# Two sets of six SBUF places for the weights of the extra expert pairs, and these pairs placed behind static pairs 3 to 10

## The reference

```python
def hier_moe(h, w_rg, b_rg, w_re, b_re, w_gate, w_up, w_down):
    g_idx = argmax(h @ w_rg + b_rg)                     # one of 4 groups of 8 experts
    e_in = (h @ w_re + b_re) of the chosen group
    top_v, top_i = top_k(e_in, 2)                       # two experts for each token
    combine = onehot(g_idx) * (g_w * softmax(top_v) at top_i)
    for every expert e:                                 # 32 experts, hidden width 256
        act = silu(h @ w_gate[e]) * (h @ w_up[e]) * combine[:, e]
        out = out + act @ w_down[e]
    return out                                          # x = x + out
```

## Time and profile before

| | us |
|---|---|
| median of 3 runs | 1676.72 (1676.46 to 1681.14) |
| span of the profiled execution | 1676.2 |
| PE busy | 1552.3 (93%) |
| DVE, ACT, POOL busy | 915.1, 761.6, 151.8 |
| 1400 to 1677 us: the router and the experts | 277 |

### The profile page before, as it was taken

The page is one execution under the profiler, slowest core; times in us unless marked ns, Lnnn a source line. Parts: engine busy times, 40 slices in busy tenths (PEclk is TensorE's granted clock), DMA queues, the critical chain, the costliest instruction groups (busy, mean ns, idle before and its releaser), DMA issues.

```text
span 1676.2 us, 23054 instructions
## 1 busy us (share of the span) xinstructions
PE 1552.3 (93%) x9664; PEld 1253.1 (75%) x9664; DVE 915.1 (55%) x1298; ACT 761.6 (45%) x1201; POOL 151.8 (9%) x202
## 2 busy tenths in 40 slices
PE   7999999999999999997999998989999999686676
PEld 6888888788887888875788888977999977333332
DVE  5545577745464554567644545796876765510102
ACT  6444554544364444466644444556755653111111
POOL 0000000100010000011100001050001000232320
PEclk9999999999999999999999999999999999798988
DMA  7555545555557455532345554432553248999996
GB/s 290 176 188 189 201 164 178 187 179 193 181 178 269 169 177 185 191 126 101 137 178 188 189 177 160 151 126 101 176 174 104 101 176 325 369 415 413 414 416 274
DMA packets 55366, 347.23 MB, mean 207 GB/s; under 512 B 10516, under 2 KB 10916, under 8 KB 15168
## 3 DMA queue, kind: packets, MB, share of 16 engines
q1 hardware_dynamic: 47520, 333.17, 53.8%
q0 software_dynamic: 7744, 12.61, 2.2%
HBM read 396.34 MB, written 9.96 MB: 242 GB/s over the span
## 4 chain that ended last, share of the span: by engine, by line
PE 78%; DVE 8%; DMA 7%; ACT 4%; issue 3%; POOL 1%; SPq 0%; DVEq 0%; POOLq 0%; ACTq 0%
PE A L424 31%; PE Y L454 20%; PE A L377 6%; PE A L362 4%; PE A L2985 4%; DMA raw<-experts,extra 2%; PE Y L3006 2%; DMA raw_whi<-experts 2%; DVE wlo L322 1%; PE A L438 1%; PE Y L393 1%; DMA raw<-stream 1%; ACT whi L311 1%; PE A L721 1%; DVE xn L521 1%
## 5 line engine op out<-in xcount | busy, mean ns | idle before, releaser
L322 DVE TENSOR_TENSOR wlo<-raw,whi 128x2048 fp32r<-128x2048 f32 (+1 forms) x226 | 496.9, 2206 | 246.2 <-ACT whi L311 245.3
L311 ACT ACTIVATE whi<-raw 128x2048 fp32r<-128x2048 f32 (+1 forms) x226 | 415.7, 1848 | 93.1 <-DMA raw<-stream 93.1
L424 PE MATMUL A<-whi,xh 128*128 128x512 f32 x768 | 308.5, 402 | 5.1 <-DVE wlo L322 5.1
L424 PE MATMUL A<-whi,xl 128*128 128x512 f32 x768 | 301.4, 392 | 0.0
L424 PE MATMUL A<-wlo,xh 128*128 128x512 f32 x768 | 300.8, 392 | 0.0
L424 PEld LDWEIGHTS A<-whi,xh 128*128 128x128 f32 x768 | 144.9, 189 | 34.2 <-DVE wlo L322 5.9
L424 PEld LDWEIGHTS A<-whi,xl 128*128 128x128 f32 x768 | 144.6, 188 | 31.7
L424 PEld LDWEIGHTS A<-wlo,xh 128*128 128x128 f32 x768 | 145.1, 189 | 28.4
L454 PE MATMUL Y<-whi,hh 128*128 128x512 f32 x352 | 140.8, 400 | 1.2 <-DVE hl L801 1.2
L454 PE MATMUL Y<-wlo,hh 128*128 128x512 f32 x352 | 139.4, 396 | 0.0
L454 PE MATMUL Y<-whi,hl 128*128 128x512 f32 x352 | 139.3, 396 | 0.0
(11 more groups left out here) (464 smaller groups left out, 2791.1 us busy)
## 6 DMA issues: line engine op xcount, KB each, us to landing
raw<-stream SPq DMA_DIRECT2D x216, 1024.0 KB, 4.9
raw_whi<-experts SPq DMA_DIRECT2D x39, 1024.0 KB, 26.5
raw<-experts SPq DMA_DIRECT2D x22, 1024.0 KB, 28.5
far<-experts SPq DMA_DIRECT2D x17, 1024.0 KB, 18.7
raw_x<-experts SPq DMA_DIRECT2D x12, 1024.0 KB, 28.5
xn<-experts SPq DMA_DIRECT2D x6, 1024.0 KB, 28.3
gains<-post_rows POOLq DMA_DIRECT2D x6, 512.0 KB, 4.7
far<-sums_at SPq DMA_DIRECT2D x4, 512.0 KB, 5.8
```

Source lines behind the costliest of these rows:

```text
L311: nc.scalar.activation(whi[:, n % RING, c], raw[:, n % RING, c], ACT.Copy).then_inc(hi_ready.sem, 1)
L322: nc.vector.tensor_tensor(wlo[:, n % RING, c], raw[:, n % RING, c], whi[:, n % RING, c].bitcast(F32), ALU.subtract).then_inc(lo_ready.sem, 1)
L424: ins = nc.tensor.matmul(bank, lhsT=lhs[:, kk, tok(t)], rhs=w[:, k, :], start=(kk == 0 and q == 0), stop=(kk == KD - 1 and q == 2))
```

## The change

The extra pairs move to stand behind static pairs 3 to 10, so at q = 4, 6, 8, ..., 18: five static pairs (11 to 15) come after the last of them. Their weights alternate between two sets of six places. Set 0 is the old one. Set 1 is `raw_whi` 2 to 4 and `ring_seam`, three places that span the end of `raw` and the beginning of `whi`; its places 6, 8, 10, 11, 14 and 16 are taken from the static loads, for which 8 places are left instead of 14. The first loads of both sets wait for the last static user of the set, every later one for the down product of the extra pair two before it. The final read of `sums_at` waits for the second-last extra pair, the last to use set 0.

```diff
-        if e in (3, 5, 6, 8, 9, 11, 12, 13):
+        if e in (3, 4, 5, 6, 7, 8, 9, 10):
             order.append(EXPERTS // 2 + len(order) - e - 1)
...
-        kept = (2, 3, 4, 5, 7, 9)
-        extra_place = [far[:, 0:3, :], raw[:, first_raw:first_raw + 3, :]]
...
-        around = [i for i in range(PLACES) if i not in kept]
+        kept = ((2, 3, 4, 5, 7, 9), (6, 8, 10, 11, 14, 16))
+        ring_seam = nc.alloc_sbuf_tensor_at("ring_seam", [P, 3, SLOT], F32, offset=place_whi - 4 * SLOT)
+        extra_place = [[far[:, 0:3, :], raw[:, first_raw:first_raw + 3, :]],
+                       [raw_whi[:, first_raw:first_raw + 3, :], ring_seam]]
...
+        around = [i for i in range(PLACES) if i not in kept[0] + kept[1]]
...
                 def weights(i):
-                    if i == 0:
-                        pool.wait_ge(slot_done.sem, first_static + static[kept[-1]] + 1)
+                    if i < 2:
+                        pool.wait_ge(slot_done.sem, first_static + static[kept[i][-1]] + 1)
                     else:
-                        pool.wait_ge(slot_done.sem, done(extra_pairs[i - 1], 2))
+                        pool.wait_ge(slot_done.sem, done(extra_pairs[i - 2], 2))
...
-                    if q == 1:
-                        weights(0)
-                    elif q in extra_pairs[:-1]:
-                        weights(extra_pairs.index(q) + 1)
+                    if q in (1, 2):
+                        weights(q - 1)
+                    elif q in extra_pairs[:-2]:
+                        weights(extra_pairs.index(q) + 2)
...
-                sp.wait_ge(slot_done.sem, done(extra_pairs[-1], 2))
+                sp.wait_ge(slot_done.sem, done(extra_pairs[-2], 2))
```

More of the change, by code:

```diff
@@ L238, in build @@
         stored = signal("stored")
-        scaled_in = signal("scaled_in")
         rows_out = signal("rows_out")
@@ L260, in build @@
         expert_loaded = [signal(f"expert_loaded{i}") for i in range(PLACES - RING)]
-        extra_loaded = signal("extra_loaded")
+        extra_loaded = [signal(f"extra_loaded{i}") for i in range(2)]
         expert_out = signal("expert_out")
@@ L2630, in build @@
         place_loaded += [next(free) for i in range(3)]
-        kept = (2, 3, 4, 5, 7, 9)
-        extra_place = [far[:, 0:3, :], raw[:, first_raw:first_raw + 3, :]]
-        assert first_raw + 3 <= RING and len(places) == PLACES
-        around = [i for i in range(PLACES) if i not in kept]
+        kept = ((2, 3, 4, 5, 7, 9), (6, 8, 10, 11, 14, 16))
+        ring_seam = nc.alloc_sbuf_tensor_at("ring_seam", [P, 3, SLOT], F32, offset=place_whi - 4 * SLOT)
+        extra_place = [[far[:, 0:3, :], raw[:, first_raw:first_raw + 3, :]],
+                       [raw_whi[:, first_raw:first_raw + 3, :], ring_seam]]
+        assert first_raw == 2 and RING == 6 and len(places) == PLACES and place_whi == place + 4 * RING * SLOT
+        around = [i for i in range(PLACES) if i not in kept[0] + kept[1]]
         static = [m for m in range(6 * PAIRS) if not is_extra(PIECES[m // 2][0])]
@@ L2646, in build @@
             if m not in loaded:
-                place_of[m] = extra_place[m % 2][:, part, :]
-                loaded[m] = extra_loaded.sem, 32 * (ORDER[q] - EXPERTS // 2 + 1)
+                i = ORDER[q] - EXPERTS // 2
+                place_of[m] = extra_place[i % 2][m % 2][:, part, :]
+                loaded[m] = extra_loaded[i % 2].sem, 32 * (i // 2 + 1)
         def load_expert(sp, m):
@@ L2883, in sparse_experts @@
             SENT = PAIRS - 2
-            yk = [extra_place[0][:, i, :].rearrange("p (t d) -> p t d", t=NT) for i in range(2)]
+            yk = [extra_place[0][0][:, i, :].rearrange("p (t d) -> p t d", t=NT) for i in range(2)]
             extra_pairs = [q for q in range(PAIRS) if is_extra(q)]
@@ L2937, in weights @@
                 def weights(i):
-                    if i == 0:
-                        pool.wait_ge(slot_done.sem, first_static + static[kept[-1]] + 1)
+                    if i < 2:
+                        pool.wait_ge(slot_done.sem, first_static + static[kept[i][-1]] + 1)
                     else:
-                        pool.wait_ge(slot_done.sem, done(extra_pairs[i - 1], 2))
+                        pool.wait_ge(slot_done.sem, done(extra_pairs[i - 2], 2))
                     for j in range(2):
-                        pool.indirect_dma_start(extra_place[j].rearrange("p a c -> p (a c)"), None, expert_rows,
+                        pool.indirect_dma_start(extra_place[i % 2][j].rearrange("p a c -> p (a c)"), None, expert_rows,
                                                 bass.IndirectOffsetOnAxis(choice.extra[:, 2 * i + j:2 * i + j + 1], 0),
-                                                bounds_check=P * EXPERTS - 1, oob_is_err=False).then_inc(extra_loaded.sem, 16)
+                                                bounds_check=P * EXPERTS - 1, oob_is_err=False
+                                                ).then_inc(extra_loaded[i % 2].sem, 16)
                 def scatter(q):
```

## The result

| | before | after |
|---|---|---|
| median | 1677.8 us (1675.2 to 1681.3, 14 runs) | 1684.1 us (1679.0 to 1688.4, 14 runs) |
| span of the profiled execution | 1676.2 us | 1684.0 us |

The ratio is 1.003 with a 95% interval of 1.002 to 1.0041, so some 5 us, with 3.4 to 6.9 as its ends; the two medians are 6.3 us apart. Forecast were 5.0 us, so it agrees within the noise, and not to the tenth. The profiled execution of the changed kernel took 1685.7 us in all, 1.6 over its own median, so its trace shows the loss a little too large.

A forecast was written before the change was run, and what follows sets the result against it. The slowest DMA engine's stream of static loads was taken as the bound; 0 + 0.5 + 4.5 + 0 = +5.0 us on 1676.2 gave 1681.2, with 0.5 for the median 1681.7; range 1676.5 to 1688.

The forecast's parts named there:

- The bound is the slowest DMA engine's stream: Experts: the slowest of 16 DMA engines, at 2.79 us a static load, sets the time, not the mean share.
- the faster rival: Tail: a ring of 8 keeps the engines together, so the stream ends sooner; 1670.9 us, chance 0.13.
- Extra weights' waits: TensorE's 23.6 us of waits for extra weights: all but the first should go, for a gain of 0.
- Late restart: Start of the experts: static load 22 goes out at 1462.00 instead of 1456.00; +4.5 us, from 2 to 6.
- The step's two deductions: Start of the experts: from 6.0 us, 0.6 off for earlier small gaps and 0.9 for rows done in the gap.
- the 4 to 6 us that were given for the last landing: End of the stream: sign that the last static load lands 4 to 6 us later than 1664.3.
- Tail: After the last landing: extra pairs earlier gain 0, at most 1.3 us, against a cold merge; +0.5, from -1.3 to +3.
- Ring of eight: Alternation of static and extra pairs: eight places keep the loads queued, 16.7 us a period against TensorE's 13.3; 0.
- my margin of 4 us: After the restart: the queue reaches to 1486.3, and the next loads' first packets come at 1482.
- POOL's wait: Extra pair 1's weights wait in POOL's queue for static load 16, ahead of a gather needed two pairs later; 0.
- The sign by which the rival was to be told: End of the stream: the engines' spread shrinks from 18 us to less than half.

The follow-up runs named there:

- e6_no_rows: Kernel before with the bounds of the experts' gathers and scatters set to 0, so nearly no row is moved; 1666.7 us, ratio 0.9932.
- e10_old_order_second_use: Changed kernel with the old order of pairs, static loads 22 to 25 using places 6, 8, 10 and 11 a second time; 1678.8 us, ratio 1.0005.
- e4_before_held: Kernel before with one wait added: static load 22 is issued only when static load 12 is done; 1683.7 us, ratio 1.003.
- e3_second_use: Changed kernel, static loads 22 to 25 reusing places 6, 8, 10, 11; extra pair 1's weights wait for load 25, not 16; 1691.4 us, ratio 1.0069.
- e1_old_order_two_sets: Changed kernel with the old positions of the extra pairs, two sets and eight places kept; 1684.0 us, ratio 1.0035.
- e7_spread_rows: Kernel before with one table changed, so that each expert's tokens are spread over its 32 row places; 1674.3 us, ratio 0.9974.

## Why the prediction was right, point by point

- **The bound is the slowest DMA engine's stream.** Shown: 12.4 us from the last static packet to the end in 11 of 13 kernels, and 4 MB less make it about 10 us shorter. The 73 loads took 1672.1 - 1469.9 = 202.2 us after, 2.77 each (1469.9 is s = 22's landing, 4.9 us behind its issue); the forecast took 2.79. The 2.4 us a load by which the faster rival had the stream end some 28 us sooner were not seen: even without rows (e6_no_rows) it was 193.4 us for 74 loads, 2.6 each.
- **Extra weights' waits: 0.** Shown: 23.6 us of waits became 0.2 with no gain, and e10_old_order_second_use has the second set without the late restart and stays at 1.0005.
- **Late restart: +4.5.** Shown. As measured in e4_before_held: +5.9 at the start, less 1.5 caught up, is +4.4. The step's two deductions (0.6 for the small gaps of before, 0.9 for rows done in the gap) come to the same 1.5; how it divides between the two no run shows. In the profile after it is 9.0 - 1.2 = 7.8, over the 4 to 6 us that were given for the last landing; 2.1 of it were there before the new wait, and other kernels with the same wait don't have them. The medians, 5 to 6 us, stand between.
- **Tail: +0.5.** It was 0: 11.9 us before and after. The merge didn't suffer from the low clock. That the sum still gave the 5.0 us of the ratio is luck at this size: 0.5 of it stood in a term that was nothing.
- **Ring of eight: 0.** Right for the changed kernel: the windows of 5 us from 1470 to 1655 have a DMA share of 0.94 to 1.07, three of them under 0.99, and the time to landing is never under 13.2. These three small dips are new (before, no window from 1465 to 1645 was under 1.00) and cost nothing that can be measured. TensorE's granted clock was 0.56 to 0.70 in 11 of these 37 windows, and the ring held all the same. But my margin of 4 us is small in earnest: a PE wait of 11.1 us opened a gap of 10 us, one of 6.7 us a small one, while one of 7.5 us in the old order cost nothing that could be measured.
- **POOL's wait: 0.** Right here, since the weights are issued right after pair 2. What I passed over is that POOL's queue is in order: in e3_second_use the same kind of wait, moved by three pairs, cost the 5 us that were to be saved and more.
- **The faster rival** thought that a shorter queue keeps the engines together, and that the end then comes sooner. Its first half came true, its second didn't. From the first to the last of the 16 engines' parts of the last static load it was 18.3 us before and 17.5 in e4_before_held, both with 14 places in the round; with eight places and the same rows it is 9.6 in the kernel after, 8.8 in e1_old_order_two_sets and 10.4 in e10_old_order_second_use. But the last part comes no sooner for it: at 1665.0 in e10_old_order_second_use, where s = 22 starts about as early as before, against 1664.3 before. So the round of eight seems to hold the quick engines back and to give the slowest nothing, though no trace here tells one engine's packets from another's. The sign by which the rival was to be told, a spread under half of 18, was therefore no sign of a gain: e1_old_order_two_sets has it and is 0.35% slower. The share still falls off ahead of the end, as these windows of the kernel after show.

```profile
1660.00:1665.00 5.00, 2.67 (x37) 1.31 (x33) 0.35 (x1) 0.65 (x2) 0.00 (x0) 0.91 0.77 321
1665.00:1670.00 5.00, 2.79 (x16) 0.66 (x16) 0.00 (x0) 0.00 (x0) 0.00 (x0) 0.77 0.97 365
1670.00:1675.00 5.00, 3.62 (x25) 1.34 (x25) 1.59 (x3) 0.87 (x2) 0.00 (x0) 0.89 0.44 179
```

What does bring the last part forward is what the slowest engine has to move. With the rows spread and 14 places (e7_spread_rows) the engines' parts lie 6.5 us apart, the last of them 7.1 us sooner than before; some of the 10 us that the rival saw in the spread were there, by another way.

## What to carry to other kernels

Find the transfer whose landing stands at a constant distance from the end, and price a change by when that transfer's stream starts, how many bytes it has, and whether it ever stands still; waits of other engines inside a full stream are free to keep or remove, as long as they don't let the ring run dry. If places are taken from a ring of prefetches, look first at the moment when the ring is filled again: which place frees next, and when. And where the DMA engines finish far apart, look for small indirect transfers whose real rows lie next to each other, and spread them. Engines that finish closer together are no gain by themselves; look at when the last one finishes.

## What the hardware showed that I had not expected

How long the slowest DMA engine works on a mix with indirect DMAs depends on where their real rows lie. Counted from the routing of this input, the real rows of all 32 experts in the eight groups of four neighbouring places were 128, 126, 117, 75, 44, 21, 1 and 0; spread they are 77, 74, 72, 67, 61, 57, 55 and 49. The rows are the same, the spread of the engines' last parts fell from 18.3 to 6.5 us and the kernel took 0.26% less. The Trainium skill has a rule that fits: DMA: Bandwidth & Descriptors, section "The descriptor swizzle", says that four neighbouring partitions go to one engine and the next four to the next. It states this for a transfer over 128 partitions, and a gather or scatter here is one: the 32 row places of two experts, in two halves of a row each, so place p lies on partitions p, p + 32, p + 64 and p + 96. The runs agree in size. If each group of four places goes to engines of its own, the fullest has 128 / 64 = 2 times the mean before and 77 / 64 = 1.2 times it when spread. By the 9.0 us of a mean engine that went in e6_no_rows, an estimate gives 18 us for taking all rows away and 7 for spreading them; measured from s = 22 to the last packet were 13.5 and 6.2. On which engine a row was moved the traces don't show, so the mapping itself is not shown.

A DMA descriptor that moves nothing isn't free either, though it is cheap: with nearly all rows left out, 5895 packets of the software queue still took 1.7% of the 16 engines' time, some 10 ns each. About half of them, 3025 packets of 4 bytes, stand in the kernel before as well (3040); the packets of 8 bytes went from 1956 to 2868. And this kernel's gathers still took 6.6 to 10.7 us to land, about as long as with their rows (6.8 to 11.9 before).
